# Token norms of a three-block transformer on one core: the state norms summed into one row per 128 tokens and spread back by a matmul, with unread matmuls around the sums

## The chip, the cores and the metric

One core of a Trainium2 chip runs the whole program. The metric is the device time of one execution in microseconds (us), the median of several runs; lower is better. The engines are PE (TensorE, matmuls; its weight loads are listed as PEld), DVE (VectorE), ACT (ScalarE), POOL (GpSimd) and SP (SyncE, whose queue issues the DMAs).

## The reference

A token state `x` (512 tokens, 1024 features) and a context `ctx` (256 tokens) go through two blocks of a mixer and a gated feed-forward, and then `x` through one block of another design. In front of every mixer and feed-forward, and at the very end, stands a norm over the 1024 features of each token:

```
def rms_norm(x, g=None):
    xf = x.astype(F32)
    y = xf * lax.rsqrt(jnp.mean(xf * xf, axis=-1, keepdims=True) + EPS)
    if g is not None:
        y = y * g.astype(F32)
    return y.astype(x.dtype)

def modulate(h, shift, scale):
    return h * (1.0 + scale) + shift
...
        h_lat = modulate(rms_norm(x, norm_g[layer, 0]), m_lat[0], m_lat[1])
        h_ctx = modulate(rms_norm(ctx, norm_g[layer, 0]), m_ctx[0], m_ctx[1])
...
    return rms_norm_2(x, final_norm_w)
```

## The kernel before

**Layout.** The state lies in SBUF with the features on the 128 partitions and the tokens in the free dimension: `x_lat` is 128 x 8 chunks x 512 tokens, `x_ctx` 128 x 8 x 256. All sums are in fp32. Every linear splits its weights and its input into a high and a low part (`fp32r` copies by ACT, remainders by POOL for weights and by DVE for the input) and sums three products on PE. Weight tiles come in one stream of DMAs through two buffers. The work is cut into blocks with a barrier of all engines between them; within a block every engine runs its own program in the order in which the code wrote it, and semaphores tie them.

**A state norm** (`norm_split`, seven of them: a before the first mixer over 768 tokens, b before the first feed-forward over 768, c before the second mixer over the 256 of the context, d over the 512 of the state beside c's linears, e before the second feed-forward, f before the third block, and one at the end written out by hand, over 512 each). ACT squares the chunks (L723; for b, d, e and f while the linear in front still runs, `squares_beside`, where DVE adds them up into `rstd` at L837). PE multiplies the squares with a 128 x 128 matrix of ones (L757, L760, L766, at the end L3527), which leaves the sum of each token on all 128 partitions of `total` in PSUM. ACT takes the root (L736), DVE the reciprocal (L779), both over all tokens. Then, chunk by chunk, DVE multiplies state, scale and `rstd` (L797), ACT adds the shift and rounds to the high part (L747), and DVE takes the low part (L785). The first matmuls of the linear behind it (L453 or L656) wait for the low part of each chunk.

**Norm a** has more on its engines. DVE makes the modulation vectors itself from weight rows that DMAs bring (L1078, some 1.3 us each, two for each vector, and L1150), six chunks of scales ahead of the norm and the others between its chunks. PE makes the first shift vector: `shift_pe` (L1260) multiplies two halves of a weight with the condition, 16 matmuls of 512 columns in all, ACT copies each half out (L1273), four small matmuls turn it (L1266), and DVE adds the bias (L1280), once before chunk 0 and once before chunk 4. The high part of chunk 0 waits for the first of these, and DVE's queue holds the L1280 in front of all that is to come. The scheme of an fp32 matmul in the trace: each is recorded as two passes.

## Time and profile before

| | us |
|---|---|
| median of 3 runs | 3054.49 |
| lowest and highest | 3046.88, 3060.53 |
| profiled execution, its own time | 3058.42 |
| its span from the first to the last instruction | 3056.6 |
| PE busy in the span | 2867.3 (94%) |
| DVE busy | 1234.3 (40%) |
| ACT busy | 1014.3 (33%) |
| POOL busy | 1239.3 (41%) |

The span is the stretch in which instructions run, the profiled execution's own time is 1.8 us longer. Busy shares are averages over many stages with different limits, so a stage has to be read from its own rows.

### The profile page before, as it was taken

Reading aid. Unit: us, or ns where it says so; the run is one execution under the profiler, and the core shown is the slowest. Engines: PE = TensorE matmul, PEld = TensorE weight load, DVE = VectorE, ACT = ScalarE, POOL = GpSimd, SP = SyncE. Lnnn points to the kernel's source line nnn. Section 1 sums busy time; section 2 is a strip of 40 time slices with the busy share of each in tenths; the row PEclk is TensorE's granted clock in tenths of the full one; section 3 lists DMA queues with packets and bytes.
Section 4 is the critical chain, followed back from the end, with each engine's and each line's share of the span. In section 5 each row is a group of like instructions: output and inputs, shape, how many; then the busy total and the mean of one; then the engine's idle time right before and its main releaser. Section 6 shows DMA issues by size and latency. Waiting matters only on the chain. (4 is left out here: it accounts for less than half of the span.)

```text
span 3056.6 us, 38956 instructions
## 1 busy us (share of the span) xinstructions
PE 2867.3 (94%) x15588; PEld 2351.7 (77%) x15588; DVE 1234.3 (40%) x1940; ACT 1014.3 (33%) x1525; POOL 1239.3 (41%) x926
## 2 busy tenths in 40 slices
PE   6999888779999999899999989999899999999998
PEld 3777787668888887889767768888678887886686
DVE  7656655651172123531174235211365454104523
ACT  3135554233211211522243332222334333325432
POOL 2221223323263234754486436444353444241342
PEclk9999988989999999999999999999899999999999
DMA  6400100411152124332342235322211111121121
GB/s 251 144 28 15 48 29 1 158 49 56 69 179 82 62 76 137 126 117 96 122 121 102 89 117 200 135 99 84 83 56 42 42 42 42 55 91 56 49 90 69
DMA packets 48700, 268.18 MB, mean 88 GB/s; under 512 B 5786, under 2 KB 7066, under 8 KB 27940
## 3 DMA queue, kind: packets, MB, share of 16 engines
q1 hardware_dynamic: 48548, 266.07, 25.0%
q8 instruction: 105, 1.72, 0.2%
q14 instruction: 47, 0.39, 0.0%
HBM read 263.95 MB, written 2.10 MB: 87 GB/s over the span
## 5 line engine op out<-in xcount | busy, mean ns | idle before, releaser
L427 POOL TENSOR_TENSOR shared_w_lo<-stage,shared_w_hi 128x512 fp32r<-128x512 f32 (+1 forms) x444 | 603.2, 1390 | 809.5 <-ACT shared_w_hi L396 809.2
L589 POOL TENSOR_TENSOR shared_w_lo<-stage,shared_w_hi 128x512 fp32r<-128x512 f32 (+2 forms) x233 | 298.1, 1309 | 610.2 <-ACT shared_w_hi L581 610.2
L396 ACT CAST shared_w_hi<-stage 128x2048 fp32r<-128x2048 f32 (+1 forms) x111 | 193.9, 1747 | 284.4 <-PE eo_banks L491 138.2
L491 PE MATMUL eo_banks<-norm_b_lo,shared_w_hi 128*128 128x512 f32 (+1 forms) x672 | 173.9, 340 | 0.0
L491 PE MATMUL eo_banks<-norm_b_hi,shared_w_hi 128*128 128x512 f32 (+1 forms) x672 | 173.5, 339 | 0.0
L913 DVE TENSOR_TENSOR ffn_hidden<-eo_banks,ffn_gate 128x512 f32<-128x512 f32 (+1 forms) x44 | 22.5, 553 | 300.7 <-PE eo_banks L491 293.0
L656 PE MATMUL two_acc<-norm_f_hi,shared_w_hi 128*128 128x512 f32 (+1 forms) x312 | 131.1, 420 | 9.6 <-DVE norm_f_lo L785 9.0
L903 ACT CAST ffn_hi<-ffn_hidden 128x768 f32 (+3 forms) x44 | 32.0, 728 | 316.6 <-DVE ffn_hidden L913 316.6
L581 ACT CAST shared_w_hi<-stage 128x1024 fp32r<-128x1024 f32 (+2 forms) x117 | 114.8, 1022 | 52.3 <-PE last_acc L656 43.7
L491 PE MATMUL f_acc<-norm_e_hi,shared_w_hi 128*128 128x512 f32 x336 | 130.8, 389 | 0.6 <-ACT ffn_gate L899 0.6
L491 PE MATMUL f_acc<-norm_e_lo,shared_w_hi 128*128 128x512 f32 x336 | 130.7, 389 | 0.0
L656 PE MATMUL two_acc<-norm_f_lo,shared_w_hi 128*128 128x512 f32 (+1 forms) x312 | 129.2, 414 | 0.6 <-DVE dn_g_cum L2982 0.6
L491 PE MATMUL eo_banks<-norm_b_hi,shared_w_lo 128*128 128x512 f32 (+1 forms) x672 | 125.7, 340 | 0.0
L491 PEld LDWEIGHTS eo_banks<-norm_b_hi,shared_w_lo 128*128 128x128 f32 x672 | 103.1, 188 | 15.8
L491 PEld LDWEIGHTS eo_banks<-norm_b_hi,shared_w_hi 128*128 128x128 f32 x672 | 103.0, 188 | 16.0
L491 PEld LDWEIGHTS eo_banks<-norm_b_lo,shared_w_hi 128*128 128x128 f32 x672 | 102.8, 188 | 15.6
L427 POOL TENSOR_TENSOR ret_w_lo<-stage,ret_w_hi 128x512 fp32r<-128x512 f32 x60 | 80.5, 1374 | 79.1 <-ACT ret_w_hi L396 79.1
L656 PE MATMUL last_acc<-norm_f_hi,shared_w_hi 128*128 128x512 f32 x256 | 102.6, 401 | 2.7 <-PEq L2892 1.8
L656 PE MATMUL last_acc<-norm_f_lo,shared_w_hi 128*128 128x512 f32 x256 | 102.1, 399 | 0.0
L491 PE MATMUL eo_banks<-ffn_lo,shared_w_hi 128*128 128x512 f32 x352 | 91.1, 340 | 0.0
L656 PE MATMUL two_acc<-norm_f_hi,shared_w_lo 128*128 128x512 f32 (+1 forms) x312 | 90.4, 415 | 0.7 <-POOL shared_w_lo L589 0.7
L491 PE MATMUL eo_banks<-ffn_hi,shared_w_hi 128*128 128x512 f32 x352 | 90.9, 339 | 0.0
(632 smaller groups left out, 7042.5 us busy)
## 6 DMA issues: line engine op xcount, KB each, us to landing
stage<-in_w_f0i SPq DMA_DIRECT2D x22, 1024.0 KB, 5.0
stage<-in_w_f1i SPq DMA_DIRECT2D x22, 1024.0 KB, 4.9
stage<-in_w_rv SPq DMA_DIRECT2D x16, 1024.0 KB, 4.9
mod_slots_a<-in_w_mod SPq DMA_DIRECT2D x24, 512.0 KB, 6.1
stage<-in_w_rqk SPq DMA_DIRECT2D x12, 1024.0 KB, 4.9
mod_slots_f<-in_w_mod SPq DMA_DIRECT2D x24, 512.0 KB, 3.6
mod_slots_e<-in_w_mod SPq DMA_DIRECT2D x24, 512.0 KB, 5.8
stage<-in_w_dqkv SPq DMA_DIRECT2D x12, 1024.0 KB, 4.9
```

The costliest lines, as they stand in the source:

```text
L396: nc.scalar.copy(w_hi[:, slot, 0:size], stage[:, slot, 0:size]).then_inc(hi_ready, 1)
L427: last = nc.gpsimd.tensor_tensor(w_lo[:, slot, part], stage[:, slot, part], w_hi[:, slot, part].bitcast(F32), ALU.subtract)
L491: mm = nc.tensor.matmul(out[0:min(P, nt), b, 0:m], w[:, k, unit[1]:unit[1] + min(P, nt)], x[:, k, s:s + m], start=begin, stop=end)
L581: last = nc.scalar.copy(w_hi[:, index % 2, part], stage[:, index % 2, part])
L589: last = nc.gpsimd.tensor_tensor(w_lo[:, index % 2, part], stage[:, index % 2, part], w_hi[:, index % 2, part].bitcast(F32), ALU.subtract)
L656: mm = nc.tensor.matmul(out[0:min(P, nt), 0:m], weights[:, k, unit[1]:unit[1] + min(P, nt)], x[:, k, s:s + m], start=begin, stop=last)
L903: nc.scalar.copy(h_hi[:, bass.ds(t, 1), :], hidden[:].rearrange("p (o n) -> p o n", o=1))\
L913: last = nc.vector.tensor_tensor(hidden[:, s:s + m], res[1][:, b, 0:m], gate[:, s:s + m], ALU.mult)
```

## The change

In each of the seven norms the ones matrix no longer has 128 columns. A 16-column strip behind the ones holds a single column of ones between zeros; a window of R columns of it, R being the number of tokens over 128 (6, 4 or 2), puts the sum of 128 tokens into row r of an R x 128 piece of PSUM and adds zeros to the others. One matmul of 512 columns becomes four of 128. Root and reciprocal then run on R x 128 elements. DVE multiplies these rows with a piece of the identity (`on_diagonal`), so that row r holds its 128 values in block r and zeros elsewhere, and PE spreads them over all partitions with a matmul of ones over R rows. DVE's products read the result in PSUM in place of `rstd` in SBUF. In norms b, e and f two matmuls of 512 columns whose result nobody reads stand ahead of the sums and two behind the spread, in norm c three and two. In norm d the spread stands one tile later than the sums.

```diff
@@ -45,7 +45,7 @@
-    out["ones"] = np.ones((P, P), f)
+    out["ones"] = np.concatenate([np.ones((P, P), f), np.tile(np.eye(11, dtype=f)[5], (P, 1)), np.zeros((P, 5), f)], axis=1)
@@ -265,7 +265,16 @@
-        ones = sb(top, "ones", [P, P])
+        ones_and_row = sb(top, "ones_and_row", [P, P + 16])
+        ones = ones_and_row[:, 0:P]
+
+        def ones_in_column(r, n):
+            return ones_and_row[:, P + 5 - r:P + 5 - r + n]
+
+        def on_diagonal(diagonal, rows, n):
+            return nc.vector.tensor_tensor(diagonal.rearrange("p (r n) -> p r n", r=n),
+                                           rows.rearrange("p (o n) -> p o n", o=1).broadcast_to([n, n, P]),
+                                           ident[0:n, 0:n].rearrange("p (r o) -> p r o", o=1).broadcast_to([n, n, P]), ALU.mult)
@@ -732,10 +745,7 @@
                 def root(act):
                     act.wait_ge(S["summed"], done["summed"] + sums)
-                    for b, (s, m, _, _) in enumerate(groups):
-                        last = nc.scalar.activation(rstd[:, s:s + m], total[:, b, 0:m], ACT.Sqrt, bias=eps_col,
-                                                    scale=1.0 / D)
-                    last.then_inc(S["root"], 1)
+                    nc.scalar.activation(rows, sum_rows, ACT.Sqrt, bias=eps_col[0:R], scale=1.0 / D).then_inc(S["root"], 1)
@@ -748,24 +758,38 @@
+                def keep_on(times):
+                    for _ in range(times):
+                        unread = total[:, 1, 0:LAT] if hold is None else hold
+                        nc.tensor.matmul(unread, ones[:], x_lat[:, 0, :], start=True, stop=True)
+
+                def spread(pe):
+                    pe.wait_ge(S["apart"], done["apart"] + 1)
+                    for b, (s, m, _, _) in enumerate(groups):
+                        mm = nc.tensor.matmul(total[:, b, 0:m], ones[0:R], squares[0:R, 0, s:s + m], start=True, stop=True)
+                    mm.then_inc(S["spread"], 1)
+
-                def of_pe(pe):
+                def of_pe(pe, with_spread=True):
                     for landed_sem, count in inputs:
                         pe.wait_ge(landed_sem, count)
+                    keep_on(hold_before)
+                    def add_rows(of, begin, end):
+                        for r in range(R):
+                            mm = nc.tensor.matmul(sum_rows, ones_in_column(r, R), of[:, r * P:r * P + P], start=begin and r == 0,
+                                                  stop=end and r == R - 1)
+                        return mm
+
...
+                    if with_spread:
+                        spread(pe)
+                    keep_on(hold_behind)
                     if shifts is not None:
                         shifts["pe"](pe)
@@ -776,8 +800,10 @@
                     dve.wait_ge(S["root"], done["root"] + 1)
-                    nc.vector.reciprocal(rstd[:], rstd[:]).then_inc(S["rstd"], 1)
+                    nc.vector.reciprocal(rows, rows).then_inc(S["rstd"], 1)
                     dve.wait_ge(S["rstd"], done["rstd"] + 1)
+                    on_diagonal(squares[0:R, 0, :], rows, R).then_inc(S["apart"], 1)
+                    dve.wait_ge(S["spread"], done["spread"] + 1)
@@ -793,9 +819,9 @@
-                                scaled[:, c % 2, s:s + m], x_of(c, s, m), a(c), rstd[:, s:s + m],
+                                scaled[:, c % 2, s:s + m], x_of(c, s, m), a(c), total[:, b, 0:m],
@@ -2297,7 +2323,8 @@
-                                home=home_b, beside=True)
+                                home=home_b, beside=True, hold=psum(norm_room, "norm_b_unread", [P, 512])[:],
+                                hold_before=2, hold_behind=2)
@@ -3524,8 +3556,12 @@
-                    nc.tensor.matmul(fg[:, 0, :], ones[:], squares[:, c % 2, :], start=c == 0, stop=c == DC - 1)\
-                        .then_inc(fn["summed"], 1)
+                    for r in range(NB):
+                        mm = nc.tensor.matmul(fg[0:NB, 0, 0:P], ones_in_column(r, NB), squares[:, c % 2, r * P:r * P + P],
+                                              start=c == 0 and r == 0, stop=c == DC - 1 and r == NB - 1)
+                    mm.then_inc(fn["summed"], 1)
+                pe.wait_ge(fn["apart"], 1)
+                nc.tensor.matmul(fg[:, 1, :], ones[0:NB], squares[0:NB, 0, :], start=True, stop=True).then_inc(fn["spread"], 1)
```

**PE in norm a.** This is PE's order from the last chunk of squares to the turning of the second shift half, before (L766 sums, L1260 shift products, L1266 turns):

```order
L766 MATMUL norm_total<-norm_squares,ones 128x512 [waits norm_squares]
L766 MATMUL norm_total<-norm_squares,ones 128x256
L1260 MATMUL shift_sums<-w_shift_hi,conds_turned 2x512 [waits shift_landed_0,shift_silu]
L1260 MATMUL shift_sums<-w_shift_hi,conds_turned 2x512 x3
L1260 MATMUL shift_sums<-w_shift_lo,conds_turned 2x512 x4
L1266 MATMUL shift_turned<-ident,shift_row 128x2 [waits shift_copied]
```

And the same place of the changed kernel, where the sums are at L778, the spread at L769, the shift products at L1286 and the turns at L1292:

```order
L778 MATMUL norm_total<-norm_squares,ones_and_row 6x128 [waits norm_squares]
L778 MATMUL norm_total<-norm_squares,ones_and_row 6x128 x5
L769 MATMUL norm_total<-norm_squares,ones_and_row 128x512 [waits norm_apart]
L769 MATMUL norm_total<-norm_squares,ones_and_row 128x256
L1286 MATMUL shift_sums<-w_shift_hi,conds_turned 2x512 [waits shift_landed_0,shift_silu]
L1286 MATMUL shift_sums<-w_shift_hi,conds_turned 2x512 x3
L1286 MATMUL shift_sums<-w_shift_lo,conds_turned 2x512 x4
L1292 MATMUL shift_turned<-ident,shift_row 128x2 [waits shift_copied]
```

Two matmuls that wait for DVE's diagonal (`norm_apart`) now stand between the sums and the shift products.

**DVE in norm a.** Before, from the last scale made ahead to the first product of a modulation row behind the norm's first chunk:

```order
L1150 TENSOR_SCALAR scale_of<-mods,small 128x1
L779 RECIPROCAL norm_rstd<-norm_rstd 128x768 [waits norm_root,context_loaded,inputs_loaded]
L797 SCALAR_TENSOR_TENSOR norm_squares<-x_lat_in,scale_of,norm_rstd 128x512 [waits mod_first_scaled,norm_rstd]
L797 SCALAR_TENSOR_TENSOR norm_squares<-x_ctx_in,scale_of,norm_rstd 128x256
L1280 TENSOR_TENSOR mods<-shift_turned,small 128x8 [waits shift_turned]
L1078 ISA mod_product_a,mods<-mod_slots_a,conds_a,small 128x1024 [waits mod_summed,mod_slot_landed_2]
```

And of the changed kernel (reciprocal L803, diagonal L275, products L823, shift L1306):

```order
L1176 TENSOR_SCALAR scale_of<-mods,small 128x1
L803 RECIPROCAL norm_rstd<-norm_rstd 6x128 [waits norm_root,context_loaded,inputs_loaded]
L275 TENSOR_TENSOR norm_squares<-norm_rstd,ident 6x768 [waits norm_rstd]
L823 SCALAR_TENSOR_TENSOR norm_squares<-x_lat_in,scale_of,norm_total 128x512 [waits mod_first_scaled,norm_spread]
L823 SCALAR_TENSOR_TENSOR norm_squares<-x_ctx_in,scale_of,norm_total 128x256
L1306 TENSOR_TENSOR mods<-shift_turned,small 128x8 [waits shift_turned]
L1104 ISA mod_product_a,mods<-mod_slots_a,conds_a,small 128x1024 [waits mod_summed,mod_slot_landed_2]
```

The reciprocal stays where it was, the diagonal is new behind it, and the first product waits for the spread where it waited for the reciprocal.

**PE at the start of norm e's block**, changed kernel (L764 unread, L778 sums, L769 spread, L462 first product of the linear):

```order
L764 MATMUL norm_total<-x_lat,ones_and_row 128x512 x2
L778 MATMUL norm_total<-norm_e_rstd,ones_and_row 4x128 [waits norm_added]
L778 MATMUL norm_total<-norm_e_rstd,ones_and_row 4x128 x3
L778 MATMUL norm_total<-norm_e_squares,ones_and_row 4x128 [waits norm_squares]
L778 MATMUL norm_total<-norm_e_squares,ones_and_row 4x128 x3
L769 MATMUL norm_total<-norm_e_squares,ones_and_row 128x512 [waits norm_apart]
L764 MATMUL norm_total<-x_lat,ones_and_row 128x512 x2
L462 MATMUL f_acc<-norm_e_hi,shared_w_hi 128x512 [waits unit_read,norm_lo,weights_hi_ready]
```

Before, the two sum matmuls of 512 columns (L757, L760) came first behind the block's barrier, and L453 followed them. Norms b and f have the same order.

## Rows read from the trace of the kernel before

**Rows 1.** The page of the whole execution, its first line.
```profile
span 3056.6 us, 38956 instructions
```

**Rows 2.** Windows: busy us (x instructions) of each engine, PEclk = granted clock.
```profile
31.00:47.40 16.40, 14.65 (x40) 3.11 (x38) 16.19 (x25) 5.58 (x10) 7.00 (x4) 1.00 0.93 358
```

**Rows 3.** Timeline, norm a: start us, us, engine, line, operation, [idle before <-releaser].
```profile
30.85 3.59 PE L1260 MATMUL shift_sums<-w_shift_hi,conds_turned 128*2 128x512 f32 x8
...
36.12 4.94 DVE L779 RECIPROCAL norm_rstd<-norm_rstd 128x768 f32<-128x768 f32 x1
...
37.91 0.57 ACT L1273 COPY shift_row<-shift_sums 2x512 f32<-2x512 f32 x1 [4.45 <-PE shift_sums L1260]
...
38.54 0.41 PE L1266 MATMUL shift_turned<-ident,shift_row 2*128 2x2 f32 x4 [0.67 <-ACT shift_row L1273]
...
41.10 0.75 DVE L797 SCALAR_TENSOR_TENSOR norm_squares<-x_lat_in,scale_of,norm_rstd 128x512 f32<-128x512 f32 x1
...
42.17 0.15 DVE L1280 TENSOR_TENSOR mods<-shift_turned,small 128x8 f32<-128x8 f32 x1
...
45.95 0.57 ACT L1273 COPY shift_row<-shift_sums 2x512 f32<-2x512 f32 x1 [2.41 <-PE shift_sums L1260]
```

**Rows 4.** Timeline, end of the first block of linears.
```profile
118.01 1.28 DVE L1078 CUSTOM_DVE_ANT_0 mod_product_a<-mod_slots_a,conds_a,small 128x1024 f32<-128x1024 f32 x1
...
119.85 0.66 PE L656 MATMUL head_acc<-norm_a_hi,shared_w_hi 128*128 128x384 f32 x1 [6.59 <-PEq L1351]
```

**Rows 5.** Timeline, norm b.
```profile
629.81 2.90 PE L757 MATMUL ffn_banks<-norm_b_rstd,ones 128*128 128x512 f32 x4 [2.52 <-PEq L2272]
...
634.28 1.05 ACT L736 ACTIVATE norm_b_rstd<-ffn_banks,small 128x512 f32<-128x512 f32 x2 [3.23 <-PE ffn_banks L760]
...
640.35 1.20 DVE L797 SCALAR_TENSOR_TENSOR norm_b_squares<-x_lat,scale_of,norm_b_rstd 128x512 f32<-128x512 f32 x1
...
645.32 0.75 DVE L797 SCALAR_TENSOR_TENSOR norm_b_squares<-x_lat,scale_of,norm_b_rstd 128x512 f32<-128x512 f32 x1
```

**Rows 6.** Timeline, norm e.
```profile
1797.97 1.10 PE L757 MATMUL norm_total<-norm_e_rstd,ones 128*128 128x512 f32 x2 [1.82 <-PEq L518]
...
1799.97 0.69 ACT L736 ACTIVATE norm_e_rstd<-norm_total,small 128x512 f32<-128x512 f32 x1 [0.75 <-PE norm_total L760]
...
1804.08 3.14 DVE L797 SCALAR_TENSOR_TENSOR norm_e_squares<-x_lat,scale_of,norm_e_rstd 128x512 f32<-128x512 f32 x2
...
1808.92 0.75 DVE L797 SCALAR_TENSOR_TENSOR norm_e_squares<-x_lat,scale_of,norm_e_rstd 128x512 f32<-128x512 f32 x1
```

**Rows 7.** Timeline, norm c.
```profile
1211.81 1.90 ACT L396 CAST shared_w_hi<-stage 128x2048 fp32r<-128x2048 f32 x1 [23.40 <-PEq L949]
...
1214.07 6.74 PE L766 MATMUL norm_total<-norm_squares,ones 128*128 128x256 f32 x16 [3.81 <-ACT norm_squares L723]
...
1221.36 0.47 ACT L736 ACTIVATE norm_rstd<-norm_total,small 128x256 f32<-128x256 f32 x1
```

**Rows 8.** Waits of PE around norm d: us, times, longest.
```profile
PE ckv_acc L495 <- POOL shared_w_lo L427: 3.3, 5, 1.1
```

**Rows 9.** Line L797 by tile: ns min/median/max, first and last start, forms.
```profile
L797 DVE SCALAR_TENSOR_TENSOR norm_d_squares<-x_lat,scale_of,norm_d_rstd x8: 739/1651/1672, 1274.9 to 1297.7; 128x512 f32<-128x512 f32 x8
```

**Rows 10.** Line L779 by tile: the reciprocals of norms a (768) and c (256).
```profile
L779 DVE RECIPROCAL norm_rstd<-norm_rstd x2: 1753/3348/4943, 36.1 to 1221.9; 128x768 f32<-128x768 f32 x1, 128x256 f32<-128x256 f32 x1
```

**Rows 11.** Timeline, a head norm: a spread from 10 rows, and its reader.
```profile
144.33 1.55 PE L1541 MATMUL head_spread<-head_rows,head_part_of 10*128 10x512 f32 x4 [0.58 <-DVE head_rows L1591]
...
145.92 1.01 DVE L1578 SCALAR_TENSOR_TENSOR head_unit<-qk,small,head_spread 128x768 f32<-128x768 f32 x1 [1.23 <-PE head_spread L1541]
```

**Rows 12.** Groups by form, PE: matmuls of 128 columns in fp32.
```profile
L3169 PE MATMUL delta_p<-upper,dn_g 128*128 128x128 f32 x64 | 7.8, 275 | 0.0
```

**Rows 13.** Timeline: DVE reads PSUM and SBUF while POOL works.
```profile
1318.34 3.78 POOL L427 TENSOR_TENSOR shared_w_lo<-stage,shared_w_hi 128x512 fp32r<-128x512 f32 x3
...
1319.38 0.69 DVE L2374 TENSOR_TENSOR ret_rope_parts<-ret_linears_acc,ret_rope 128x512 f32<-128x512 f32 x1 [16.65 <-PE ret_linears_acc L491]
```

More of the change, by code:

```diff
@@ L688, in feature_units, with norm_split @@
             return [("F", c, segs) for c in range(0, nt, P)]
-        norm_sem = {k: sem("norm_" + k) for k in ("squares", "summed", "root", "rstd", "scaled", "hi", "lo", "added")}
+        norm_sem = {k: sem("norm_" + k) for k in ("squares", "summed", "root", "rstd", "apart", "spread", "scaled", "hi", "lo", "added")}
         norms = [0]
-        def norm_split(x_of, groups, hi, lo, inputs=(), scales=None, home=None, shifts=None, scales_ahead=0, beside=False):
+        def norm_split(x_of, groups, hi, lo, inputs=(), scales=None, home=None, shifts=None, scales_ahead=0, beside=False,
+                       hold=None, hold_before=0, hold_behind=0, counts=None):
             n = norms[0]
@@ L702, in norm_split @@
             sums = 1 if beside else DC
+            R = T // P
             def source(scope):
@@ L754, in of_pe @@
                     if beside:
                         pe.wait_ge(S["added"], done["added"] + DC - 2)
-                        for b, (s, m, _, _) in enumerate(groups):
-                            nc.tensor.matmul(total[:, b, 0:m], ones[:], rstd[:, s:s + m], start=True, stop=False)
+                        add_rows(rstd, True, False)
                         pe.wait_ge(S["squares"], done["squares"] + DC)
-                        for b, (s, m, _, _) in enumerate(groups):
-                            mm = nc.tensor.matmul(total[:, b, 0:m], ones[:], squares[:, (DC - 1) % 2, s:s + m],
-                                                  start=False, stop=True)
@@ L762, in of_pe @@
-                        mm.then_inc(S["summed"], 1)
+                        add_rows(squares[:, (DC - 1) % 2, :], False, True).then_inc(S["summed"], 1)
                     for c in range(0 if beside else DC):
                         pe.wait_ge(S["squares"], done["squares"] + c + 1)
-                        for b, (s, m, _, _) in enumerate(groups):
-                            mm = nc.tensor.matmul(total[:, b, 0:m], ones[:], squares[:, c % 2, s:s + m],
-                                                  start=c == 0, stop=c == DC - 1)
@@ L807, in of_dve @@
                     low(DC - 1)
-                return dict(act=of_act, pe=of_pe, dve=of_dve, root=root, take_hi=take_hi, ready=S["lo"], first=done["lo"], beside=beside)
-            for k, m in (("squares", DC), ("summed", sums), ("root", 1), ("rstd", 1), ("scaled", DC), ("hi", DC),
+                return dict(act=of_act, pe=of_pe, spread=spread, dve=of_dve, root=root, take_hi=take_hi, ready=S["lo"], first=done["lo"], beside=beside)
+            for k, m in (("squares", DC), ("summed", sums), ("root", 1), ("rstd", 1), ("apart", 1), ("spread", 1), ("scaled", DC), ("hi", DC),
                          ("lo", DC), ("added", DC - 2 if beside else 0)):
@@ L2347, in norm_d_pe @@
                 if t == 2:
-                    norm_d["pe"](pe)
+                    norm_d["pe"](pe, with_spread=False)
+                elif t == 3:
+                    norm_d["spread"](pe)
             def norm_d_dve(dve, t):
@@ L3371, in program @@
             "delta_hi", "delta_lo", "dilated_hi", "dilated_lo", "a_done", "projected", "b_gate", "b_gated", "merged",
-            "merged_hi", "merged_lo", "x_done", "squares", "summed", "root", "rstd", "scaled")}
+            "merged_hi", "merged_lo", "x_done", "squares", "summed", "root", "rstd", "apart", "spread", "scaled")}
         def ga_unit(dve, t, u, done, out):
@@ L3681, in _ @@
                 act.wait_ge(fn["summed"], DC)
-                nc.scalar.activation(rstd[:], fg[:, 0, :], ACT.Sqrt, bias=eps_col, scale=1.0 / D).then_inc(fn["root"], 1)
+                nc.scalar.activation(rstd[0:NB, 0:P], fg[0:NB, 0, 0:P], ACT.Sqrt, bias=eps_col[0:NB], scale=1.0 / D).then_inc(fn["root"], 1)
             @block.gpsimd
```

25 lines of the change are left out of this document (16 added, 9 removed).

## Prediction

> **What bounds the kernel now.** I read the page first, for the span [rows 1], then the windows and the timeline around each of the seven state norms, then the waits, and last the groups for the price of single operations. PE is busy for most of the span, so a norm costs where PE stands still for it: from the end of the sums through root, reciprocal and the first product to the first low part. Behind that point DVE makes the chunks (product and low part), and PE keeps up with it even at the half clock, so the end of each norm moves with the start of DVE's products. The reader is to see this path in norm e: sums from 1797.97, root at 1799.97, first product at 1804.08 [rows 6]. Norm a is different. There DVE is busy for 16.19 of the 16.40 us in which it starts, and PE for 14.65 [rows 2]: PE makes the shift vector from 30.85 on, at once behind the sums, while DVE still makes scales; the reciprocal begins only at 36.12, the first product at 41.10, and the shift is added at 42.17, long after it was turned at 38.54 + 0.41 [rows 3]. DVE goes on without a pause worth naming to 118.01, and PE then waits 6.59 us for the end of that block [rows 4]. So whatever moves DVE's chain in norm a moves the block's end.
>
> **The path behind the sums.** Before, over 512 tokens: 1804.08 - 1799.97 = 4.11 us [rows 6]; norms f and last have the same two operations. Over 768: 640.35 - 634.28 = 6.07 [rows 5]. Over 256: 0.47 [rows 7] + 1.75 [rows 10] + 0.07 = 2.3.
> After: the root of 128 columns, from 0.47 for 256 [rows 7] and 0.69 for 512 [rows 6], is 0.36. The reciprocal takes 1753 ns for 256 columns and 4943 for 768 [rows 10], 6.23 ns a column, so 0.95 for 128. The diagonal is an elementwise product of 512 elements, 0.69 [rows 13]; about 0.95 for 768 and 0.42 for 256. The spread has a near copy in the head norms: from 10 rows to 128 partitions over 768 tokens, and its reader starts 145.92 - 144.33 = 1.59 after it [rows 11]. Two passes of 256 columns less, at 7.8 / 64 = 0.12 for a pass of 128 [rows 12], make 1.15 for 512 and 0.75 for 256. Handoffs add 0.18. Sums: 3.33 for 512 (saves 0.78), 4.03 for 768 (saves 2.04), 2.66 for 256 (loses 0.36). PE stands still for two or three us before the spread; should it then run at half clock, the spread takes about as long again in its columns: 0.85, 1.28 or 0.43 more. These are the two bounds, and I take the full clock for b, e, f and the last, since their sums and unread matmuls lie close before it.
>
> **The products from PSUM.** The Trainium skill speaks against this edit. First the rows: a DVE product with one operand in PSUM takes 0.69 for 512 elements while POOL works beside it [rows 13], and the head norm's product over 768 from PSUM takes 1.01 [rows 11]. Norm d's products with both in SBUF take 1651 ns in the median and 739 at the least [rows 9], and norm e's first two took 3.14 together [rows 6]. The page "VectorE: DVE Perf Modes", section "Rules for kernel authors", advises to copy matmul output from PSUM to SBUF first if many operations read it, as eight or sixteen do here. By that rule a copy near the root's size would be worth having on each path; by the rows there is nothing to win back, and the operand's move to PSUM takes a collision with POOL away. The rest goes by the rows. What remains contended is the low part, with two operands in SBUF. In norm e, product 0 to product 2 took 1808.92 - 1804.08 = 4.84 [rows 6]; two products of 0.75 and a low part of up to 1.75 make 3.3, and POOL, now earlier than DVE's chain by less, gives 0.4 back in the next low part: -1.1. In norm b the same stretch took 645.32 - 640.35 = 4.97 [rows 5] and becomes about 4.05: -0.9.
>
> **The unread matmuls.** They stand first in PE's program of the block, and PE in norms b, e and f finds its data ready when the block opens. In norm e two matmuls of 512 in fp32, with the handoff, take from 1797.97 to 1799.97 [rows 6], so two in front put everything off by 1.9. In norm b PE opens at half clock: four passes over 768 take 2.90 [rows 5] where the head norm's take 1.55 [rows 11]; there the unread ones take the slow stretch on themselves (about 3.3) and the sums follow at 2.9 instead of 4.47 in all: +1.8. The ones behind the spread end before the first low part is there, and since DVE sets the pace after that, I cost and credit them at nothing; if that cover were gone they would cost 1.9. **Sums by rows** take passes of 0.12 for 128 columns: 16 passes 1.95 against 1.9, +0.1 for each of b, d, e and f, and for the eight chunks of the last norm, which lie between PE's own matmuls, 0.3 to 0.8, say 0.5.
>
> **Norm by norm.**
> *a:* reciprocal at 36.12 as before, since DVE's scales set it; + 0.95 + the diagonal, 0.95 alone or up to twice that beside POOL, say 1.4: PE gets it at 38.5. PE has then been idle for some 6 us and spreads at half clock, 2.8: 41.3. The first product comes when it did (41.10). But only now do the shift matmuls begin, 10 us later than 30.85: twice 3.59 [rows 3], and 0.5 for a slow start, end at 49.0; 1.0 later they are turned (38.95 less 30.85 + 2 x 3.59), and DVE adds the shift at about 50.0 instead of 42.17. All DVE work of the block is queued behind that addition, and ACT's high part of chunk 0 waits for it: **+7.8**. The second half's copy (45.95 before [rows 3]) comes at about 57.7, before DVE has got to the chunk that needs it. Bounds: everything at full clock, +5.6; the diagonal doubled and the slow stretch long, +8.9.
> *b:* +1.8 + 0.1 - 2.04 - 0.9 = **-1.0** (half-clock spread: -0.2).
> *c:* PE waits 3.81 for the squares and then runs the sums at half clock, 6.74 for 16 passes of 256 [rows 7]. The block opens with ACT's 1211.81 [rows 7]; three unread matmuls, 2.8 us from there, end at 1214.6, 0.4 behind the first squares, and the sums then run at a pace of 0.5 a chunk: root at about 1219.4 instead of 1221.36. With the longer path behind it: **-1.5**, or +0.2 where the clock falls in spite of them.
> *d:* the sums and the spread lie in PE's stream of the context's linears: +0.1 + 1.0. But PE waits there 3.3 us for POOL's low parts [rows 8], and POOL runs beside the doubled products of [rows 9]; with these gone I take 2.0 of it: **-0.9**, between +1.1 and -2.2.
> *e:* +1.9 + 0.1 - 0.78 - 1.1 = **+0.1** (half clock: +0.9). *f:* no POOL work beside it: +1.9 + 0.1 - 0.78 = **+1.2** (+2.1). *Last:* -0.78 + 0.5 = **-0.3** (+0.9).
> Sum: 7.8 - 1.0 - 1.5 - 0.9 + 0.1 + 1.2 - 0.3 = +5.4. Against the profiled execution's 3058.42 this is 3063.8; that execution lies 3.9 above the median of the runs, and from 3054.49 the sum gives **3060**.
>
> **The rivals.**
> *Slower: the shift matmuls in norm a run at half clock throughout.* They hold only two columns of weights, and begin behind a long idle stretch. Against it: before, with the same form, the granted clock was 1.00 over the whole stretch [rows 2], though they began right behind busy sums. Then the first half ends at 41.3 + 14.4, the shift is added at 56.7, +14.5; the second copy comes at 71 instead of 45.95, of which some 5 is slack: +20. With the others' -2.4 the time is 3072. It decides if the clock stays low for over 8 us.
> *The delay in norm a isn't carried:* DVE might have waited for modulation rows later anyway. For it, PE has its own work in that block; against it, DVE is the last to end the block [rows 4] and hardly waits. Then -2.4: 3052.
> *The unread matmuls pay:* the clock stays full behind the norms, too. In norm f the first linear's chunks leave PE mostly idle, and the matmuls behind the last chunk run at half clock before; at full clock some 2 us come back, and 1 or 2 elsewhere: 3056.
> *Faster by more than that:* norm a's stall must be absent and POOL's relief in norm d must reach its bound, -4.9 in all: 3050, still within 0.5% of before.
>
> **How the numbers follow.** A difference under 0.5%, 15.3 us here, is about what a measurement of this kernel can't tell from none. Chances: the forecast 0.71, the slower rival 0.08, the delay not carried 0.09, the unread ones pay 0.09, the rest 0.03. With every norm at its lower bound the sum is 5.6 - 1.0 - 1.5 - 2.2 + 0.1 + 1.2 - 0.5 = about +2, with every one at its upper 8.9 - 0.2 + 0.2 + 1.1 + 0.9 + 2.1 + 0.9 = +14: 3056 to 3068, the forecast's own range. Down to 3050 it takes in the two rivals below it. That leaves out the slower rival and the rest. Slower by over 0.5% holds the slower rival, less than half of which lies under the mark, and part of the rest: 0.07. Faster by over 0.5% has only the rest: 0.04.
>
> **What would show it.** In the changed profile: norm a's shift matmuls begin near 41 and the bias is added near 50, with DVE idle before it; the block ends near 127 instead of 119. Reciprocals of 0.95, roots of 0.36, a spread of 0.9 to 1.7 in norm e; its sums begin 1.9 later in the block, and its first products take 0.75 beside POOL. Norm c's sums run at full clock. The prediction is wrong if DVE doesn't wait in norm a, if products from PSUM slow down beside POOL, or if PE's clock is half through the shift.

## The result, and the profile after

The changed kernel takes 3067.98 us (median of 15 runs, 3061.37 to 3074.24), the kernel before 3053.76 beside it (15 runs, 3034.59 to 3062.03): a ratio of 1.0052, with a 95% interval of 1.0037 to 1.0068. It is slower by 14.2 us in the medians; the forecast was +5.4 us, a time of 3060.

The page of the changed kernel, its first lines (span; busy time, share and instructions):

```profile
span 3072.0 us, 39425 instructions
...
PE 2896.4 (94%) x15820; PEld 2364.2 (77%) x15820; DVE 1208.3 (39%) x1947; ACT 1011.0 (33%) x1523; POOL 1233.3 (40%) x926
```

The span is 15.4 us longer than in [rows 1]; DVE lost 26 us of busy time, PE gained 29. Norm a, timeline of the changed kernel (columns as in [rows 3]):

```profile
36.00 0.93 DVE L803 RECIPROCAL norm_rstd<-norm_rstd 6x128 f32<-6x128 f32 x1
36.96 1.89 DVE L275 TENSOR_TENSOR norm_squares<-norm_rstd,ident 6x768 f32<-6x768 f32 x1
...
38.90 2.92 PE L769 MATMUL norm_total<-norm_squares,ones_and_row 6*128 6x512 f32 x4 [7.97 <-DVE norm_squares L275]
...
41.75 5.83 PE L1286 MATMUL shift_sums<-w_shift_hi,conds_turned 128*2 128x512 f32 x8
41.86 0.75 DVE L823 SCALAR_TENSOR_TENSOR norm_squares<-x_lat_in,scale_of,norm_total 128x512 f32<-128x512 f32 x1 [3.02 <-PE norm_total L769]
...
47.42 3.60 PE L1286 MATMUL shift_sums<-w_shift_lo,conds_turned 128*2 128x512 f32 x8
...
51.68 0.41 PE L1292 MATMUL shift_turned<-ident,shift_row 2*128 2x2 f32 x4 [0.67 <-ACT shift_row L1299]
...
52.12 0.17 DVE L1306 TENSOR_TENSOR mods<-shift_turned,small 128x8 f32<-128x8 f32 x1 [9.12 <-PE shift_turned L1292]
...
130.68 0.66 PE L665 MATMUL head_acc<-norm_a_hi,shared_w_hi 128*128 128x384 f32 x1 [7.04 <-PEq L1377]
```

PE stands idle for 7.97 us until the diagonal is there, the shift matmuls begin behind the spread, and DVE stands idle for 9.12 us in front of the addition of the shift. It comes at 52.12 instead of 42.17 [rows 3], and the matmul behind the block at 130.68 instead of 119.85 [rows 4]: +10.8. Windows of the same stretch (columns as in [rows 2]):

```profile
30.90:38.90 8.00, 0.04 (x1) 0.00 (x0) 7.81 (x12) 1.82 (x3) 6.88 (x4) 0.82 0.99 417
38.90:46.00 7.10, 7.10 (x10) 1.77 (x11) 1.14 (x2) 0.00 (x0) 0.00 (x0) 0.50 0.76 295
46.00:60.00 14.00, 12.67 (x36) 2.77 (x34) 7.40 (x14) 2.61 (x5) 0.00 (x0) 0.99 0.11 39
```

The granted clock falls within the idle stretch, is 0.50 (1.2 GHz) over the spread and the first of the shift matmuls, and is back at 46. Norms b, c, e, timeline of the changed kernel:

```profile
644.82 1.96 PE L764 MATMUL norm_b_unread<-x_lat,ones_and_row 128*128 128x512 f32 x4 [2.52 <-PEq L2298]
...
649.53 0.36 ACT L748 ACTIVATE norm_b_rstd<-ffn_banks,small 6x128 f32<-6x128 f32 x1 [3.47 <-PE ffn_banks L778]
...
653.49 0.75 DVE L823 SCALAR_TENSOR_TENSOR norm_b_squares<-x_lat,scale_of,ffn_banks 128x512 f32<-128x512 f32 x1 [1.65 <-PE ffn_banks L769]
...
657.78 0.75 DVE L823 SCALAR_TENSOR_TENSOR norm_b_squares<-x_lat,scale_of,ffn_banks 128x512 f32<-128x512 f32 x1
...
1226.98 4.35 PE L778 MATMUL norm_total<-norm_squares,ones_and_row 128*2 128x128 f32 x32
...
1231.99 0.36 ACT L748 ACTIVATE norm_rstd<-norm_total,small 2x128 f32<-2x128 f32 x1
...
1234.84 0.87 DVE L823 SCALAR_TENSOR_TENSOR norm_squares<-x_ctx,scale_of,norm_total 128x256 f32<-128x256 f32 x2 [1.06 <-PE norm_total L769]
...
1811.51 1.95 PE L764 MATMUL norm_total<-x_lat,ones_and_row 128*128 128x512 f32 x4 [1.82 <-PEq L527]
...
1815.34 0.36 ACT L748 ACTIVATE norm_e_rstd<-norm_total,small 4x128 f32<-4x128 f32 x1 [2.60 <-PE norm_total L778]
...
1817.44 1.76 PE L769 MATMUL norm_total<-norm_e_squares,ones_and_row 4*128 4x512 f32 x2 [2.13 <-DVE norm_e_squares L275]
...
1819.23 1.41 DVE L823 SCALAR_TENSOR_TENSOR norm_e_squares<-x_lat,scale_of,norm_total 128x512 f32<-128x512 f32 x2 [1.85 <-PE norm_total L769]
...
1821.87 0.75 DVE L823 SCALAR_TENSOR_TENSOR norm_e_squares<-x_lat,scale_of,norm_total 128x512 f32<-128x512 f32 x1
```

In b the path from root to first product is 3.96 instead of 6.07 us [rows 5], in e 3.89 instead of 4.11 [rows 6]. Behind it the stretch from the first to the third product of 512 elements is 2.64 in e instead of 4.84, and 4.29 in b instead of 4.97. Norm d, line by tile and PE's waits:

```profile
L823 DVE SCALAR_TENSOR_TENSOR norm_d_squares<-x_lat,scale_of,norm_d_total x8: 742/748/751, 1288.6 to 1306.3; 128x512 f32<-128x512 f32 x8
```
```profile
PE ckv_acc L504 <- POOL shared_w_lo L436: 3.5, 3, 2.2
```

The products fell from 1651 to 748 ns [rows 9], and PE waits for POOL no less than before: 3.5 against 3.3 [rows 8]. The last norm, timeline of before and then of the changed kernel, two sums that lie between PE's own matmuls:

```profile
3031.36 1.02 PE L3527 MATMUL last_banks<-final_squares,ones 128*128 128x512 f32 x2
...
3037.70 1.02 PE L3527 MATMUL last_banks<-final_squares,ones 128*128 128x512 f32 x2
```
```profile
3047.08 1.04 PE L3560 MATMUL last_banks<-final_squares,ones_and_row 128*4 128x128 f32 x8
...
3053.71 1.04 PE L3560 MATMUL last_banks<-final_squares,ones_and_row 128*4 128x128 f32 x8
```

The sum itself reads 1.02 and 1.04, but the pace from one to the next is 6.34 before and 6.63 after: what it costs shows in the stream around it.

**Stage by stage.** The same matmul is looked up in two traces, and the difference of its two starts says how far one kernel is behind. The change of this difference over a stage, in us against the first profile of before (edges are times of before; some records are missing from each trace, so that a value can be off by 0.5; 1850 to 2170 is 0.0 in every column and left out; e1 and so on are the experiments below). At the matmul of [rows 4] itself, which every trace has, the differences are +10.8, +10.4 (e12), -0.4 (e1), +0.1 (e2), -0.5 (e3), +9.2 (e4), 0.0 (e5) and -1.2 (e8):

| stage | changed | again (e12) | before again (e1) | e2 | e3 | e4 | e5 | e8 | e10 | e11 |
|---|---|---|---|---|---|---|---|---|---|---|
| a: 0 to 119 | +10.8 | +10.6 | +0.1 | 0.0 | -0.3 | +9.3 | +0.4 | -1.1 | +0.3 | +0.1 |
| 119 to 620 | +4.2 | -5.9 | +4.3 | -4.5 | +0.4 | -5.9 | -6.2 | +4.6 | -5.5 | -4.7 |
| b: to 700 | -2.6 | -3.5 | -1.6 | -1.1 | -1.0 | -0.4 | -2.9 | -4.5 | -2.8 | -1.6 |
| 700 to 1205 | 0.0 | -9.5 | 0.0 | 0.0 | 0.0 | 0.0 | 0.0 | 0.0 | 0.0 | 0.0 |
| c, d: to 1330 | -0.6 | +1.4 | +0.2 | +0.3 | 0.0 | -0.1 | -0.3 | +2.0 | -0.8 | -0.2 |
| 1330 to 1790 | +1.8 | +1.7 | +0.6 | +0.7 | +0.7 | +0.5 | +0.6 | +1.1 | +0.6 | +0.2 |
| e: to 1850 | -0.4 | -0.4 | 0.0 | -0.4 | -0.4 | 0.0 | -2.3 | -2.3 | -2.3 | 0.0 |
| f: 2170 to 2240 | +0.9 | -0.1 | +0.1 | -0.1 | +0.9 | -0.8 | -0.4 | -0.4 | -0.4 | +0.1 |
| 2240 to 2995 | +0.1 | +2.8 | -3.2 | +2.8 | +4.7 | +7.5 | +7.9 | +8.0 | +3.4 | +0.1 |
| last | +1.2 | +1.3 | -0.4 | +1.5 | +1.8 | -0.2 | +1.6 | -7.3 | -6.4 | -6.5 |

The stages with norms sum to +9.3 in the changed kernel and +9.2 in its second profile (e12). The other four hold nothing that was changed, and there one program differs from itself by up to 10 us (first column against second).

### The profile page after: what moved, and what is told of

Same layout as the page of the kernel before. It is cut to its first block and busy times, and to the rows that moved or that the text cites. A ratio compares the mean times of both kernels' runs of the same rounds, so it can differ in the third digit from the quotient of the medians.

```text
span 3072.0 us, 39425 instructions
## 1 busy us (share of the span) xinstructions
PE 2896.4 (94%) x15820; PEld 2364.2 (77%) x15820; DVE 1208.3 (39%) x1947; ACT 1011.0 (33%) x1523; POOL 1233.3 (40%) x926
```

## The experiments

Each ran beside the kernel before on the same chip (22 to 35 runs of it, 6 to 12 of each kernel). Lines with + and - are against the kernel named. A ratio is that to the kernel before which ran beside it, with its 95% interval; the experiments ran on four chips, so kernels of different groups (e1 to e4, e5 to e8, e9 to e12, e13 to e15) are compared by their ratios.

**e1, the kernel before once more.** No edit.

> The kernel before, unchanged, profiled a second time. Question: the changed kernel lost 4.4 us between 510 and 562 us, in a stage that the change doesn't touch, because the tensor clock was at half there in other places than before. If the place of the half-clock stretches is luck of the execution (theory A), this second profile of the kernel before differs from the first by whole microseconds in that stage too (its span 3045 to 3062, the ratio 1.000 within 0.2%). If it belongs to the program (theory B), every stage repeats the first profile within 0.3 us, and the span is 3056 to 3058.

Measured: ratio 0.9996 (0.998 to 1.0011), span 3056.6 us, the same as the first. The windows of the stage in question, the first profile of before and then the second:

```profile
505.00:517.00 12.00, 12.00 (x59) 12.00 (x58) 6.24 (x7) 11.12 (x15) 0.70 (x1) 0.50 0.00 0
517.00:531.00 14.00, 11.28 (x169) 8.35 (x167) 9.34 (x17) 6.47 (x11) 10.54 (x7) 1.00 0.01 2
```
```profile
505.00:517.00 12.00, 12.00 (x59) 12.00 (x58) 6.26 (x7) 11.10 (x15) 0.68 (x1) 0.50 0.00 0
517.00:531.00 14.00, 11.70 (x104) 9.26 (x103) 6.78 (x15) 4.59 (x8) 10.04 (x6) 0.74 0.00 1
```

In this stretch the two agree to 0.02 us up to 517 (at 118 us they were 0.35 apart); then one execution has the full clock and the other stays at half for a while longer, and it is 4 us behind at 531. Later it gets 1.6 back in norm b and 3.2 behind 2240. That both spans come to 3056.6 is chance: the 12 runs of this kernel go from 3043.2 us, at a mean granted clock of 0.972, to 3064.2, at 0.964. Theory A holds: the 4.2 us that the changed kernel lost in this stage prove nothing about the change.

**e2, norm a's spread behind the first turning** (against the changed kernel).

```diff
@@ of_pe
+                    if shifts is not None:
+                        shifts["pe"](pe, (0,))
                     if with_spread:
                         spread(pe)
                     keep_on(hold_behind)
                     if shifts is not None:
-                        shifts["pe"](pe)
+                        shifts["pe"](pe, (1,))
```

> The changed kernel with one thing moved: in norm a the spread stands behind the first half of the shift vector (16 passes and the turning) and ahead of the second. Theory 1, the place of the spread in PE's program cost norm a its 10.4 us: the shift is added near 42 to 43 again instead of 52.12, the first matmul of the linear starts near 47.5 to 48, the spread takes 1.5 at full clock, and the time falls by 10 us, to about 3058 (ratio to before 1.001 to 1.003). Theory 2, the longer path (diagonal, spread, products from PSUM) costs it whatever the order: the shift is added early, but the first matmul still starts later than 54, and the time falls by less than 4 us.

Measured: 3057.35, ratio 1.0007 (0.9988 to 1.0026). Its timeline:

```profile
39.19 1.55 PE L769 MATMUL norm_total<-norm_squares,ones_and_row 6*128 6x512 f32 x4
...
40.79 0.75 DVE L825 SCALAR_TENSOR_TENSOR norm_squares<-x_lat_in,scale_of,norm_total 128x512 f32<-128x512 f32 x1 [1.65 <-PE norm_total L769]
...
41.84 0.16 DVE L1308 TENSOR_TENSOR mods<-shift_turned,small 128x8 f32<-128x8 f32 x1
```

The spread waits for nobody, runs at full clock, and the shift is added at 41.84, before the 42.17 of before. The matmul behind the block comes at 119.93 instead of 119.85. Theory 1 holds: norm a's loss hung on the place of the spread; behind the turning, its longer path costs norm a nothing.

**e3, all but norm a changed,** and **e4, norm a alone.** In e3 norm a calls `norm_split` in its form of before, in e4 the other six norms do, without unread matmuls.

> The changed kernel with norm a in the form of before (ones of 128 columns, root and reciprocal over 768, products from SBUF), all else changed. Reading the two traces norm by norm gives b -2.6, c and d together -0.6, e -0.3, f +1.0, the last +1.2: -1.3 in all. If nothing else differs: 3052 to 3053, ratio 0.9996 (0.998 to 1.001). If the 6 us that went elsewhere (the stages at 510 to 562 and at 1500 to 1600) belong to the other norms' change: 3058.

> The kernel before with norm a alone in the changed form, no unread matmuls. Theory 1: +10.4 from norm a, 3064, ratio 1.0034. If the shift by 10 us also brings the half-clock stretches of the stage at 510 to 562 with it (+4.4, as in the profile of the changed kernel): 3069, ratio 1.0049. If the delay in norm a is partly recovered later: under 3060.

Measured: e3 3055.08, ratio 0.9995 (0.9978 to 1.0013), e4 3066.58, ratio 1.0043 (1.0028 to 1.0057). The loss is in norm a, and the other six together are within what can be told from none. In e4's table column the stage of a shows +9.3 (9.2 at the matmul of [rows 4]), and the stage behind it -5.9 where the changed kernel had +4.2: the half-clock stretches don't come with the delay.

**e5, no unread matmuls at all** (against e2: every `hold_before` and `hold_behind` gone).

> The previous version (spread behind the first turning in norm a) without any unread matmul. Its trace is read norm by norm, from the block's start to the first low part, against the changed kernel. Theory 1, the two in front only cost where PE's data is ready: root in norm e 1.9 earlier in its block (2.0 after the sums' start instead of 3.9), the same in f, so e and f gain 1.9 each; in norm b the sums take the slow stretch themselves and nothing is gained or 0.3; in norm c the sums fall to half clock, 6.5 us for 32 passes instead of 4.35, and c loses 1.7 or more. Sum -2. Theory 2, they keep the clock up: the first linears behind them run longer at half clock without them, and the end of each first linear moves later by 2 us each in b, c, e and f, +6 or more.

Measured: 3048.7, ratio 0.9988 (0.9973 to 1.0003). In its trace:

```profile
1204.96 5.68 PE L778 MATMUL norm_total<-norm_squares,ones_and_row 128*2 128x128 f32 x32 [3.81 <-ACT norm_squares L736]
...
1789.18 1.03 PE L778 MATMUL norm_total<-norm_e_rstd,ones_and_row 128*4 128x128 f32 x8 [1.82 <-PEq L527]
...
1794.38 1.41 DVE L825 SCALAR_TENSOR_TENSOR norm_e_squares<-x_lat,scale_of,norm_total 128x512 f32<-128x512 f32 x2 [1.21 <-PE norm_total L769]
```

Norm e's stage is 1.9 shorter than in e2 (from its first matmul to its first product 5.20 us instead of 7.72, of which the spread, 1.12 at full clock instead of 1.76, is 0.6). Norm f's is 0.3 shorter, where theory 1 had 1.9, and norm b's is 1.8 shorter, where it had nothing or 0.3. Norm c's sums are slower, 5.68 against 4.35, as theory 1 has it, but by 1.3 and not 1.7 or more, and the stage of c and d is no longer for it (-0.3, +0.3 in e2). No stage of a norm is longer than in e2 by more than the 0.5 that can't be read. Theory 2 is out: the unread matmuls gave back nothing that could be found. They did raise the mean granted clock, 0.971 over e2's runs against 0.968 over e5's (0.967 and 0.968 for the kernel before beside them), but e5 has the lower ratio: a higher mean clock was no gain here.

**e6, the spread row copied to SBUF first** (against e2).

```diff
@@ of_dve
                     dve.wait_ge(S["spread"], done["spread"] + 1)
+                    for b, (s, m, _, _) in enumerate(groups):
+                        last = nc.vector.tensor_copy(rstd[:, s:s + m], total[:, b, 0:m])
...
-                                scaled[:, c % 2, s:s + m], x_of(c, s, m), a(c), total[:, b, 0:m],
+                                scaled[:, c % 2, s:s + m], x_of(c, s, m), a(c), rstd[:, s:s + m],
```

> The version with the spread behind the first turning, and in each of the six norms ahead of the last DVE copies the spread row from PSUM to SBUF once and the products read SBUF. Theory 1, the operand in PSUM is what spared the products the collision with POOL: in norm e the copy adds 0.65 and the first two products take 3.1 again instead of 1.41, +2.4; in norm b +0.9 to +1.9; c +0.4, f +0.7; about +5 in all. Theory 2, a copy pays where many operations read it (eight to sixteen here): each later product is shorter by more than 0.08, and the norms end no later than without the copy. Theory 3, only the copy's own time: +0.7 per norm, +3, the products as before.

Measured: 3066.88, ratio 1.0049 (1.0031 to 1.0067). Norm e, timeline of e6:

```profile
1803.50 0.69 DVE L810 COPY norm_e_rstd<-norm_total 128x512 f32<-128x512 f32 x1 [1.80 <-PE norm_total L769]
...
1804.22 2.43 DVE L829 SCALAR_TENSOR_TENSOR norm_e_squares<-x_lat,scale_of,norm_e_rstd 128x512 f32<-128x512 f32 x2
```

The two products take 2.43 us instead of 1.41. Norm d's products, beside POOL, show it best; line by tile in e6 (the median is 748 ns in the changed kernel and in e2):

```profile
L829 DVE SCALAR_TENSOR_TENSOR norm_d_squares<-x_lat,scale_of,norm_d_rstd x8: 752/1670/1792, 1273.2 to 1294.5; 128x512 f32<-128x512 f32 x8
```

The stages of a, b, e and f are 1.1, 0.7, 2.0 and 0.5 longer than in e2, that of c and d 0.3 shorter: +4.0 together, where theory 1 had about 5. It holds in direction and nearly in size; 2 and 3 are out, since the products are slower and not as before. By the ratios e6 is slower than e2 by more, 0.42% or 12.8 us; each of the two ratios is uncertain by some 0.2%, or 6 us, and nothing in the profile shows the rest.

**e7, norms d and the last in the form of before** (against e2).

> The version with the spread behind the first turning, with norm d and the last norm in the form of before. Theory 1, sums by rows cost the last norm 0.30 for each chunk that lies between PE's own matmuls: the pace of the last linear is 6.34 a chunk again instead of 6.64, -2.4, and the longer root and reciprocal give 0.8 back: the end is 1.2 to 1.5 earlier against the changed kernel's. Norm d: +0.6 in the changed kernel, so the first matmul of the next block comes 0.6 earlier. Rival: the pace of 6.64 comes from somewhere else (the clock, weights), and stays.

Measured: 3053.42, ratio 1.0002 (0.9987 to 1.0017). The pace of the last linear is 6.34 again, and from its first state update to the end the kernel takes 59.7 us as before, instead of 61.2 in e2: 1.5 shorter, as theory 1 has it; the rival is out. The stage of c and d is 0.5 shorter than in e2, which is less than it differs between two profiles of the changed kernel. Norm d's products take 1654 ns again, and PE's wait for POOL in e7 is

```profile
PE ckv_acc L504 <- POOL shared_w_lo L436: 3.6, 5, 1.1
```

with slow products as with fast ones.

**e8, the last norm's squares added up by DVE, nothing unread in front in b, e, f** (against e2).

```diff
@@ DVE, last norm
+                for c in range(1, DC - 1):
+                    more.upto(at["wo"] + 24 * (c + 1) + 12)
+                    dve.wait_ge(fn["squares"], c + 1)
+                    wait(dve, fn["added"], c - 1)
+                    nc.vector.tensor_tensor(rstd[:], rstd[:], squares[:, c % 2, :], ALU.add).then_inc(fn["added"], 1)
```

> The version with the spread behind the first turning, with two edits: no unread matmul in front of the sums of b, e and f (those behind stay, c keeps all), and in the last norm DVE adds up the squares of seven chunks (it stands idle for 5.9 us between its state updates), so that PE sums only twice at the end. If PE's sums between its own matmuls are what sets the pace there: 5.5 a chunk instead of 6.64, 7 times 1.16 less = -8.1 against the changed kernel. Norms e and f -1.9 each, b 0 to -1.9, unless their clock falls for it (+1 each). Time 3042 to 3046, ratio 0.996 to 0.9975. If DVE's additions hold up the state updates instead: no more than -2 in the last norm.

Measured: 3046.67, ratio 0.9974 (0.9954 to 0.9993). Timeline of e8, two state updates with DVE's addition between them:

```profile
3036.97 0.75 DVE L3448 SCALAR_TENSOR_TENSOR x_lat<-last_acc,ada,x_lat 128x512 f32<-128x512 f32 x1 [3.30 <-PE last_acc L665]
...
3038.42 0.69 DVE L3654 TENSOR_TENSOR final_rstd<-final_rstd,final_squares 128x512 f32<-128x512 f32 x1 [0.70 <-ACT final_squares L3725]
...
3042.41 0.75 DVE L3448 SCALAR_TENSOR_TENSOR x_lat<-last_acc,ada,x_lat 128x512 f32<-128x512 f32 x1 [3.30 <-PE last_acc L665]
```

The pace is 5.44 us a chunk, and the stage of the last norm is 8.4 shorter than in the changed kernel (-7.3 against +1.2, before rounding). The addition lies in DVE's idle time.

**e9, PE kept busy in norm a** (the changed kernel, seven unread matmuls between sums and spread).

> The changed kernel with seven more unread matmuls of 512 columns in norm a, between its sums and its spread, where PE stands idle for 8 us. Theory: of the 9.95 us by which the shift is added late, the clock makes 1.4 in the spread (2.92 instead of 1.55) and 2.2 in the first shift matmuls (5.83 instead of 3.60), the order makes the rest. Then the granted clock is 1.00 from 30 to 46, the shift is added near 48.5 instead of 52.12, and the time falls by 3.6. Rival: the half clock has nothing to do with PE's idle stretch, and both stay as they are.

Measured: 3064.38, ratio 1.0036 (1.0013 to 1.0059). Windows and timeline of e9:

```profile
38.00:46.00 8.00, 7.66 (x19) 1.94 (x20) 1.43 (x3) 0.00 (x0) 1.41 (x1) 1.00 0.77 297
```
```profile
38.34 1.55 PE L769 MATMUL norm_total<-norm_squares,ones_and_row 6*128 6x512 f32 x4 [0.53 <-DVE norm_squares L275]
39.82 3.60 PE L1288 MATMUL shift_sums<-w_shift_hi,conds_turned 128*2 128x512 f32 x8
...
47.96 0.17 DVE L1308 TENSOR_TENSOR mods<-shift_turned,small 128x8 f32<-128x8 f32 x1 [6.89 <-PE shift_turned L1294]
```

The clock stays full, spread and the first half of the shift take 1.55 and 3.60 us, and the stage of a costs 6.7 instead of 10.8. Of these 4.2 us (unrounded) 0.6 is a reciprocal that came earlier here, at 35.42, and 3.6 the half clock's part in norm a's loss; the order made the rest.

**e10, the best of these** (e8 with norm d in the form of before), and **e11, the kernel before with DVE's additions in the last norm alone.**

> The version with the spread behind the first turning, no unread matmuls in front in b, e and f, the last norm's squares added up by DVE, and norm d in the form of before. By the stages of the profiles so far: a 0, b -4.4 to -2.6, c -1.7, d 0, e -2.3, f -0.4, last -7.3: -16 to -18, 3036 to 3039, ratio 0.9945 (0.993 to 0.996).

> The kernel before with one edit: in the last norm DVE adds up the squares of seven chunks, PE sums twice at the end; root, reciprocal and products over 512 columns as before. Eight sums between PE's matmuls take 0.86 a chunk before (6.34 against 5.48), so seven of them less: -6.0, ratio 0.998. How much of the best version's gain is the rows' is what is left over.

Measured: e10 3043.69, ratio 0.9968 (0.9945 to 0.9991), faster than both kernels, but by the ratio 9.8 us against the kernel before and not the 16 to 18 expected: its norms sum to -12.3 against before, with b at -2.8 where e8 had -4.5. e11 3045.08, ratio 0.998 (0.9959 to 1.0001), its last stage -6.5 as expected. So half of e10's gain or more is the additions', which have nothing to do with the rows; e11's own interval just holds 1.

**e12, the changed kernel once more.**

> The changed kernel, unchanged, profiled a second time. The norms should repeat within 1 us each (a +10.4 to +10.8 at the end of its block, b -2.6, e -0.35, f +1, last +1.2); the stages between them, where nothing was changed, may differ by some us either way, as between the two profiles of the kernel before. Median 3066 to 3070, ratio 1.004 to 1.006.

Measured: 3067.39, ratio 1.0049 (1.0026 to 1.0073), but its profiled execution has a span of 3055.0. The norms repeat within 2 us (c and d +1.4 instead of -0.6), and 9.5 us were won from 700 to 1205, where PE never stops and the clock is full in both. Windows of the changed kernel and of e12, and the row of one group from each page:

```profile
1000.00:1050.00 50.00, 50.00 (x285) 43.36 (x284) 5.93 (x9) 10.54 (x12) 14.22 (x13) 1.00 0.18 63
```
```profile
1000.00:1050.00 50.00, 50.00 (x291) 44.10 (x289) 5.94 (x9) 10.55 (x12) 15.19 (x13) 1.00 0.19 63
```
```profile
L500 PE MATMUL eo_banks<-norm_b_hi,shared_w_hi 128*128 128x512 f32 (+1 forms) x672 | 174.1, 340 | 0.0
```
```profile
L500 PE MATMUL eo_banks<-norm_b_hi,shared_w_hi 128*128 128x512 f32 (+1 forms) x672 | 171.5, 336 | 0.0
```

**e13 to e15, a known delay in norm a of the kernel before:** 6, 12 and 24 unread matmuls between its sums and its shift matmuls.

> The kernel before with one edit: six unread matmuls of 512 columns between the sums of norm a and its shift matmuls, 5.4 us at 0.45 a pass. No rows, no spread, clock full: only the shift comes late. It was turned 3.2 us before DVE added it, so it is added at 44.5 instead of 42.17 and the block ends 2.3 later. If a late shift costs just that: +2.3, ratio 1.0008. If every delay costs the stages behind it more: over +4.

> The same with twelve unread matmuls, 10.8 us: the shift is added at 49.9, 7.7 late. If a late shift costs just that: +7.7 in the profile at the end of the block, ratio 1.0025. If a delay of this size costs the later stages 4 to 5 us more by the place in which their half-clock stretches then fall (the medians of the changed kernel lie 14 to 15 us over before, the norms in its traces sum to 9): ratio 1.004 or more.

> The same with twenty-four, 21.6 us: the shift is added at 60.6, 18.4 late; ratio 1.006 if the delay is passed on one to one, 1.0075 or more if something is added behind, under 1.005 if part of it is caught up.

Measured: the shift is added at 44.13, 50.30 and 60.81, the matmul of [rows 4] comes 1.9, 8.0 and 19.2 later. The ratios are 1.0026 (1.0005 to 1.0048), 1.0041 (1.0022 to 1.0059) and 1.0103 (1.0076 to 1.0131), in us +7.9 (1.5 to 14.7), +12.5 (6.7 to 18.0) and +31.4 (23.2 to 40.0). The first two intervals hold the bare delay, the third, of six runs, doesn't. Nothing is caught up, and something seems to be added behind. Which stage adds it the single profiles can't say: e13 and e14 have spans of 3050.3 and 3048.6, shorter than before, through stages that nobody changed (e14 too won 9.5 from 700 to 1205).

## Why the prediction was wrong

**What failed is the size of the term of norm a.** The mechanism was right: spread ahead of the shift, reciprocal held by DVE's scales (36.00, forecast 36.12), first product about when it came before (41.86), DVE idle before the addition, the delay carried to the block's end (e14: 8.1 late at the addition, 8.0 at the end). It was priced at +7.8 with a bound of +8.9, and measured +10.8 and +10.4. The step is "and 0.5 for a slow start": the first half of the shift's passes took 5.83 us instead of 3.59, so 2.2 and not 0.5, since the half clock that the prediction gave to the spread went on for some 4 us behind it. The spread itself was priced at half clock (2.8, measured 2.92), the diagonal at 1.4 (1.89: the upper bound, beside POOL). Together these put the addition at 52.12 instead of the 50.0 forecast. The remaining 0.9 lies behind the addition: it came 9.95 late, the block's end 10.8. The same 0.9 is in e4, e9 and e12, 0.4 in e2, none in e13 and e14 and 0.5 in e15, whose norms have the form of before; the prediction had no term for it, and what it is stays open. The rival of the half clock "throughout" named the right danger and bound it to an all-or-nothing condition; e9 shows the middle, 3.6 us. The other errors in part cancel each other.

**Norm b** was -1.0: -2.6 and -3.5 against the first profile of before, -1.0 and -1.9 against the second. The path behind the sums is as summed (3.96 for 4.03), the products gave 0.7 for 0.9. The root came 0.2 later in its block, not 1.9, since the clock was full at its opening this time (1.00 from 640 to 650; 0.79 from 627 to 635 before). With one and the same code this stage was -2.6, -3.5 and, in e2, -1.1.

**Norm c:** its root was forecast at 1219.4. It came at 1231.99, and its block opened at 1224.20 instead of 1211.81 [rows 7], so 1219.6 on before's time: right. But the spread ran at half clock, and the path from root to first product cost 2.85 instead of 0.36 + 0.95 + 0.42 + 0.75 + 0.18 = 2.66: -1.2 at the first product. **Norm d** was -0.9 by a relief that never reached PE: DVE's operations halved, PE's waits for POOL stayed, and they stayed the same with the slow products of e7 (3.6). Together the stage of c and d is -0.6 and +1.4 where -2.4 stood. **Norm e** +0.1: -0.4 in both profiles; 1.83 later by the unread matmuls, 0.2 back on the path (half clock in the spread, the upper bound), 2.2 instead of 1.1 by the products. **Norm f** +1.2: +0.9 and -0.1.

**The last norm** was -0.3 and is +1.2 and +1.3. "Say 0.5" for eight sums by rows failed: at 0.29 a chunk between PE's own matmuls seven cost 2.0, and in e7, with the sums of before, the pace is back at 6.34. The row of the sum (1.04 against 1.02) didn't show that.

**Products from PSUM:** the choice against the rule of the Trainium skill's page "VectorE: DVE Perf Modes", section "Rules for kernel authors", was right by e6: the copy costs its 0.69 us and brings the collision back. The Trainium skill's page "SBUF — State Buffer", section "Who interferes with whom", says that a DVE instruction with at most one input in SBUF, outside its two-port modes, does not contend with GpSimd (POOL), and that one with two contends with a GpSimd instruction that reads SBUF; 748 ns with an operand in PSUM against 1651 (before) and 1670 (e6) with both in SBUF, beside POOL, agrees.

**Of the unread matmuls** the prediction said that those in front cost 1.9 in e and f and those behind nothing; e5 and e8 agree in e (-1.9 without them), and less in f (0.3 to 1.3). The rival in which they pay is out. The last rival's -4.9 does not follow from its terms, which give -3.7, or 3051; it had next to no chance in the sum.

**The rest of the difference.** The norms' stages sum to +9.3, the forecast to +5.4, the medians differ by 14.2 (interval 11.3 to 20.8). The four stages without a norm made +6.0 in the changed kernel's first profile and -10.9 in its second, so the profile does not settle the last 5 us. Luck of the 15 runs is not a good account of it, since e12's 12 runs, beside 35 others of the kernel before, repeat the ratio (1.0049). That a late norm a costs more than its delay in the medians is what e15 shows, by six runs, and e13 and e14 allow; but e6, whose norm a is hardly late, has the same excess (ratio 1.0049, norms' stages about +4), so lateness can't be all of it. By which stage it comes stays open. The measured 3067.98 lies 8 us above the forecast: 3.9 are in the norms' stages, some 5 have no term, and the kernel before came out 0.7 below the 3054.49 that the sum started from. That it falls just inside the forecast's own range, 3056 to 3068, is luck: norm a and the last norm lie above their upper bounds (8.9 and 0.9), norm b below its lower (-1.0). The prediction took one execution's stages as fixed and gave the runs around it no width.

## What to carry to other kernels

Work that is put on PE ahead of an independent task, as the spread ahead of the shift, must be priced with that task's whole path, and at the clock that the wait in front of it leaves behind; putting it one task later cost nothing here (e2). An operation between another stream's matmuls is priced by the pace of that stream, not by its own row. Before a difference of a few us between two profiles is explained, the same kernel has to be profiled twice.

## What the runs showed that was not expected

One program, executed twice, agrees to 0.02 us from 505 to 517 us and is 4 apart at 531, with a granted clock of 1.00 in one and 0.74 in the other from 517 to 531. Two of seventeen profiles (e12, e14) ran the feed-forward from 700 to 1205 1.9% faster, 291 matmul passes in 50 us instead of 285, with PE busy throughout and the granted clock at 1.00 in both. What chooses between the two paces is open.
